# First block's attention: a pair's two heads multiply with the values in the two column halves of the array

## What is computed

```
q  = (rms_norm(c_q)  @ w_uq ).reshape(..., 8, 64 + 32)      # rope on the last 32
kv = (rms_norm(c_kv) @ w_ukv).reshape(..., 8, 64 + 64)      # k_nope, v
s  = (q_nope @ k_nope.T + q_rope @ k_rope.T) * 96 ** -0.5   # causal, the meta tokens always seen
p  = softmax(s)
out = p @ v                                                 # per head [256 queries, 64]
merged = concat(rms_norm(out of 8 heads), rms_norm(conv)) @ w_out
```

## Time and profile before

| | before |
|---|---|
| median of 3 runs | 684.5 us (684.24 to 686.52) |
| profiled execution, its span | 681.9 us |
| PE busy | 633.8 us (93%) |
| PE weight loads busy | 479.1 us (70%) |
| DVE busy | 356.7 us (52%) |
| ACT busy | 294.6 us (43%) |
| POOL busy | 51.3 us (8%) |
| DMA | 180.73 MB, mean 265 GB/s |

### The profile page before, as it was taken

The page is one execution under the profiler, slowest core; times in us unless marked ns, Lnnn a source line. Parts: engine busy times, 40 slices in busy tenths (PEclk is TensorE's granted clock), DMA queues, the critical chain, the costliest instruction groups (busy, mean ns, idle before and its releaser), DMA issues.

```text
span 681.9 us, 10213 instructions
## 1 busy us (share of the span) xinstructions
PE 633.8 (93%) x4027; PEld 479.1 (70%) x4027; DVE 356.7 (52%) x689; ACT 294.6 (43%) x562; POOL 51.3 (8%) x76
## 2 busy tenths in 40 slices
PE   8999899998998766879899999999999999999996
PEld 5979788842543320334389999998788888888884
DVE  5687664731031020110188876757856666666665
ACT  6855572431011010100185755564665555555554
POOL 3100101100010000000049000000000000000001
PEclk9999999999999997879999999999999999999999
DMA  8956328999999999999997333355535555555101
GB/s 341 420 227 245 130 118 346 395 382 426 426 389 424 421 420 420 422 421 420 423 420 295 131 125 124 124 186 186 185 128 193 193 195 194 200 194 186 62 1 62
DMA packets 26286, 180.73 MB, mean 265 GB/s; under 512 B 3184, under 2 KB 3312, under 8 KB 5120
## 3 DMA queue, kind: packets, MB, share of 16 engines
q1 hardware_dynamic: 25200, 177.60, 66.1%
q10 hardware_dynamic: 1040, 2.50, 0.9%
HBM read 179.04 MB, written 1.05 MB: 264 GB/s over the span
## 4 chain that ended last, share of the span: by engine, by line
PE 69%; DMA 16%; DVE 8%; ACT 5%; issue 2%; SPq 0%; POOLq 0%; POOL 0%; ACTq 0%; DVEq 0%
PE ps L1612 66%; DMA ring<-stream_dram 15%; PE ps L1615 3%; DVE ring_r L408 3%; ACT single L401 1%; DMA h<-x_dram 1%; DVE work L1547 1%; ACT work L887 1%; DVE work L1550 1%; DVE h L1600 0%; DVE work L1603 0%; ACT turned L892 0%; ACT work_r L883 0%; DVE extra_r L503 0%; DVE work L1428 0%
## 5 line engine op out<-in xcount | busy, mean ns | idle before, releaser
L1612 PE MATMUL ps<-turned,single 128*128 128x256 f32 (+2 forms) x944 | 231.2, 326 | 1.6 <-ACT work L664 0.8
L1612 PE MATMUL ps<-turned,ring_r 128*128 128x256 f32 (+1 forms) x648 | 179.7, 281 | 0.0
L1612 PEld LDWEIGHTS ps<-turned,single 128*128 128x128 f32 x944 | 156.2, 189 | 18.5 <-issue 2.0
L408 DVE TENSOR_TENSOR ring_r<-ring,single 128x1024 fp32r<-128x1024 f32 (+1 forms) x132 | 160.3, 1236 | 14.1 <-ACT single L401 13.9
L401 ACT ACTIVATE single<-ring 128x1024 fp32r<-128x1024 f32 (+1 forms) x132 | 134.0, 1046 | 0.1
L1612 PEld LDWEIGHTS ps<-turned,ring_r 128*128 128x128 f32 x648 | 121.1, 188 | 0.4
L1612 PE MATMUL ps<-ring,work 128*32 128x512 f32 (+2 forms) x462 | 69.9, 611 | 16.0 <-DMA ring<-stream_dram 13.9
L1612 PEld LDWEIGHTS ps<-single 128*128 128x128 f32 x257 | 38.7, 190 | 34.0 <-issue 22.8
L1612 PE MATMUL ps<-single,turned 128*128 128x512 f32 (+3 forms) x208 | 59.2, 364 | 2.4 <-DVE turned L1227 1.5
L1612 PE MATMUL ps<-single 128*128 128x512 f32 (+1 forms) x257 | 55.7, 356 | 2.9 <-DVE single L1439 1.9
L1612 PE MATMUL ps<-single,work_r 128*128 128x512 f32 x176 | 56.2, 392 | 0.0
(11 more groups left out here) (260 smaller groups left out, 719.1 us busy)
## 6 DMA issues: line engine op xcount, KB each, us to landing
ring<-stream_dram SPq DMA_DIRECT2D x145, 1024.0 KB, 12.4
work<-stream_dram SPq DMA_DIRECT2D x12, 1024.0 KB, 12.5
turned_w<-stream_dram SPq DMA_DIRECT2D x4, 1024.0 KB, 14.4
extra<-stream_dram SPq DMA_DIRECT2D x2, 1024.0 KB, 11.4
ring<-stream_dram SPq DMA_DIRECT2D x2, 832.0 KB, 8.4
h<-x_dram SPq DMA_DIRECT2D x2, 512.0 KB, 4.9
gain<-gains_dram ACTq DMA_DIRECT2D x2, 512.0 KB, 10.4
yields<-stream_dram SPq DMA_DIRECT2D x1, 1024.0 KB, 13.0
```

Source lines behind the costliest of these rows:

```text
L408: dve.tensor_tensor(ring_r[:, place, a], ring[:, place, a], w_hi[k % HIGHS][:, a].bitcast(F32), ALU.subtract).then_inc(s["wlo_done"], 1)
L1612: return pe.matmul(o, lhsT, rhs, start=start, stop=stop, **kw)
```

## The change

The values of a pair no longer have zeros between the heads: `v1` has one tile for each of the three key tiles (meta first), 64 columns for each head. `values(hp)` is called once for a pair. It multiplies head j's 64 columns to the rows 64 j to 64 j + 63 of the bank, with both query tiles streamed as 256 columns for the meta keys and the first 128 keys, and the second query tile alone (128 columns) for the last 128 keys: six fp32 matmuls, the two heads taking turns. The transposed probabilities of all four units of a pair are kept (`pt1` and the new `pt_meta`). `values(u // 4 - 1)` stands at u = 4, 8 and 12, ahead of `turn_probs(u)`, and that of the last pair behind the loop; what `turn_probs` cuts out of a row is shifted so that the meta keys come apart. POOL's three memsets and the waits on `pad_done` 2 go.

```diff
-            act.wait_ge(s["o_ps"], 4 * (hp + 1))
+            act.wait_ge(s["o_ps"], hp + 1)
...
-                        sp.wait_ge(s["o_ps"], 2 * HEADS)
+                        sp.wait_ge(s["o_ps"], HEADS // 2)
...
-                    if w == 0:
-                        act.wait_ge(s["pad_done"], 2)
                     act.wait_ge(s["pt_ps"], w + 1)
-                    full_k = P if w % 2 == 0 else 2 * P
-                    act.activation(pt1[:, w % 2, 0:full_k], ps[:, 3 + w % 2, 0:full_k], ACT.Copy)
-                    act.activation(pt1[0:META, w % 2, full_k:full_k + P], ps[0:META, 3 + w % 2, full_k:full_k + P],
+                    j, i = (w // 2) % 2, w % 2
+                    act.activation(pt1[:, j, i * P:(2 * i + 1) * P], ps[:, 3 + w % 2, 0:(i + 1) * P], ACT.Copy)
+                    act.activation(pt_meta[0:META, j, i * P:(i + 1) * P], ps[0:META, 3 + w % 2, 2 * P:3 * P],
                                    ACT.Copy).then_inc(s["pt_sb"], 1)
...
-            pool.memset(pm1[:, :, COLS:3 * P], 0.0).then_inc(s["pool_step"], 1)
...
-            pool.memset(pt1[:, 0, P:2 * P], 0.0).then_inc(s["pool_step"], 1)
...
-            pool.memset(pt1[:, 1, 2 * P:3 * P], 0.0).then_inc(s["pad_done"], 1)
...
-                for k in range(2 + u % 2):
-                    last = turn(ps[:, 3 + u % 2, k * P:(k + 1) * P], pm1[:, u % 3, k * P:(k + 1) * P])
+                for k in range(1 + u % 2):
+                    last = turn(ps[:, 3 + u % 2, k * P:(k + 1) * P], pm1[:, u % 3, META + k * P:META + (k + 1) * P])
...
-                last.then_inc(s["pt_ps"], 1)
-
-            def values(u):
-                hd, i = u // 2, u % 2
-                pe.wait_ge(s["pt_sb"], u + 1)
-                if hd >= 4 and u % 4 == 0:
-
-                    pe.wait_ge(s["att_low"], hd // 2 - 1)
-                o = ps[:, 6 + (hd // 2) % 2, i * P:(i + 1) * P]
-                c = (3 * (hd // 2) + hd % 2) * VD
-                for k in range(2 + i):
-
-                    last = mm(o, v1[k][:, c:c + 2 * VD], pt1[:, i, k * P:(k + 1) * P], u % 4 == k == 0,
-                              u % 4 == 3 and k == 1 + i, skip_group_check=True)
+                turn(ps[:, 3 + u % 2, 2 * P:3 * P], pm1[:, u % 3, 0:P]).then_inc(s["pt_ps"], 1)
+
+            def values(hp):
+
+                pe.wait_ge(s["pt_sb"], 4 * hp + 4)
+                if hp >= 2:
+                    pe.wait_ge(s["att_low"], hp - 1)
+                for k in range(NT + 1):
+                    for j in range(2):
+                        c = (2 * hp + j) * VD
+                        probs = pt_meta[:, j, :] if k == 0 else pt1[:, j, (k - 1) * TOK:TOK + (k - 1) * P]
+                        last = mm(ps[j * VD:(j + 1) * VD, 6 + hp % 2, (k // 2) * P:TOK], v1[:, k, c:c + VD], probs,
+                                  k == 0, k == NT, skip_group_check=True)
                 last.then_inc(s["o_ps"], 1)
...
+                if u and u % 4 == 0:
+                    values(u // 4 - 1)
                 turn_probs(u)
-                if u:
-                    values(u - 1)
...
-            values(2 * HEADS - 1)
+            values(HEADS // 2 - 1)
```

More of the change, by code:

```diff
@@ L205, in two_blocks @@
         xn = cut(NT, D)
-        v1_last = cut(3 * VD * HEADS // 2)
+        pt_meta = cut(2, TOK)
         top[0] = (NT + 1) * D
@@ L218, in two_blocks @@
         kT = cut(HEADS, COLS)
-        v1_whole = cut(NT, 3 * VD * HEADS // 2)
-        v1 = [v1_whole[:, 0, :], v1_whole[:, 1, :], v1_last]
+        v1 = cut(NT + 1, VD * HEADS)
         assert top[0] <= ASIDE_FROM + 4 * SLOT
@@ L535, in two_blocks @@
         TILES = [(0, META, 0), (1, P, META), (2, P, META + P)]
+        VALUE_TILES = TILES[1:] + TILES[:1]
         block = ctx.enter_context(nc.Block())
@@ L691, in _ @@
             act.wait_ge(s["pad_done"], 1)
[L692 to L696, removed]
+            for j, (i, m, _) in enumerate(VALUE_TILES):
+                act.wait_ge(s["v_ps"], j + 1)
+                act.activation(v1[0:m, i, :], ps[0:m, 4 + j, :], ACT.Copy).then_inc(s["v_sb"], 1)
             for hp in range(0, HEADS // 2, 2):
@@ L964, in power @@
                 return pool.tensor_tensor(rs, ms, cst[:, C_NHALF:C_NHALF + 1].to_broadcast([P, rs.shape[1]]), ALU.pow)
-            for a, value in ((kT[QKD:P, :, :], 0.0), (ones_s, 1.0), (qT[QKD:P, :, :], 0.0), (v1_last, 0.0)):
+            for a, value in ((kT[QKD:P, :, :], 0.0), (ones_s, 1.0), (qT[QKD:P, :, :], 0.0), (pt_meta, 0.0)):
                 pool.memset(a, value).then_inc(s["pool_step"], 1)
@@ L969, in _ @@
                 pool.wait_ge(s["pool_step"], steps[0])
-            pool.memset(v1_whole, 0.0).then_inc(s["pad_done"], 1)
+            pool.memset(v1[:, 0, :], 0.0).then_inc(s["pad_done"], 1)
             pool.wait_ge(s["pad_done"], 1)
@@ L980, in _ @@
             power(msz, rsz).then_inc(s["rz_done"], 1)
-            pool.wait_ge(s["qr_done"], NT)
-            pool.wait_ge(s["t3_ps"], 3)
-            pool.memset(pm1[:, :, COLS:3 * P], 0.0).then_inc(s["pool_step"], 1)
-            steps[0] += 1
-            pool.wait_ge(s["pool_step"], steps[0])
-            pool.memset(pt1[:, 0, P:2 * P], 0.0).then_inc(s["pool_step"], 1)
-            steps[0] += 1
-            pool.wait_ge(s["pool_step"], steps[0])
-            pool.memset(pt1[:, 1, 2 * P:3 * P], 0.0).then_inc(s["pad_done"], 1)
             def add_squares(to, other):
@@ L1740, in _ @@
                 last.then_inc(s["q_ps"], 1)
-            for i, m in enumerate((P, P, META)):
-                pe.wait_ge(s["q_sb"], (1, 1, 2)[i])
-                mm(ps[0:m, 4 + i, :], ckvT[:, i * P:i * P + m], wkv[:, HEADS * NOPE:HEADS * (NOPE + VD)], True, True
+            for j, (_, m, c) in enumerate(VALUE_TILES):
+                pe.wait_ge(s["q_sb"], (1, 1, 2)[j])
+                mm(ps[0:m, 4 + j, :], ckvT[:, c:c + m], wkv[:, HEADS * NOPE:HEADS * (NOPE + VD)], True, True
                    ).then_inc(s["v_ps"], 1)
@@ L1765, in _ @@
             pe.wait_ge(s["v_sb"], 3)
-            pe.wait_ge(s["pad_done"], 2)
             def scores(u):
```

## The result

| | before | changed |
|---|---|---|
| median, five runs each on one chip | 684.46 us (683.67 to 686.52) | 688.19 us (686.43 to 688.59) |
| profiled execution, its span | 681.9 us | 684.6 us |

The changed kernel takes 1.0051 of the time before, with a 95% interval of 1.0037 to 1.0065: about 3.5 us slower. The forecast of 684.6 us, with a range up to 686.8, is wrong: 688.19 lies above it. An unchanged copy of the changed kernel on a second chip gave 1.0031 (1.0019 to 1.0042); the two intervals meet at 1.0037 to 1.0042. The profiled execution of after took 686.43 us and is the fastest of its five. It lies 1.8 us above its span, as in every profiled run for which both are known. So of the 2.6 us that the forecast put around the span of before only 1.8 lie there; the rest is scatter between executions.

The account below looks back on a forecast made before the run. PE was taken to bound the attention's second half, with waits in the first. Terms +0.28, -0.31, -0.62 and +0.73 sum to +0.08 us: span 682.0, plus 2.6 gives 684.6 us, range 682.8 to 686.8.

Parts of the forecast that it names:

- A block, 1.40 us: One pair's value matmuls on PE in column halves: 1.09 us plus 0.31 for switching parts, against 2.24 before.
- Term 1: Up to unit 4's transposes: values(1) and values(2) go (-1.12 us), block 0 comes (+1.40); conv_share start also later: +0.28.
- Term 2: 83.69 us to unit 13's transposes: values(6) to values(11) go, two blocks come, new wait of 0.25 us: -0.31 us.
- the clock falls: Rival: about 2.5 us idle ahead of conv_share lowers PE's clock in the attention; 686.3 to 688.0 us; chance 0.12.
- Term 3: Unit 13's to unit 15's transposes: values go, new wait of 0.5 us for unit 15's probabilities: -0.62 us.
- Term 4: End of the attention: the last block (1.40 us) stands where values(15) (0.67) stood, behind unit 15's copy: +0.73 us.
- (a): 48 value records in place of 80; those of 256 columns start in twos; a block takes 1.1 us without edges.
- (b): The first record behind a block comes 0.1 us late, and its transposes too.
- (d): PE waits 0.25 us ahead of unit 11's transposes and 0.5 us ahead of unit 15's.
- (c): The first conv_share starts at about 84.0 us in place of 83.69.
- (e): The last block starts about 1.14 us behind unit 15's transposes, and mix_share within 0.5 us of 105.8.
- All of it shows: Rival: switches cost nothing and the 4.6 us of PE work saved over four blocks all count; 679.9 us; chance 0.09.

Follow-up runs that it names:

- kernel 1: Changed kernel plus four unused fp32 matmuls of 272 columns in PE's idle time ahead of the first conv_share; 685.24 us, ratio 1.0006.
- kernel 8: kernel 7 with the third pair's block behind unit 15's transposes and ACT's and DVE's work on that pair behind it; 681.42 us, 0.9955.
- kernel 5: Kernel before, with values(5) moved from ahead of the first conv_share to behind it; 688.06 us, 1.0052.
- kernel 7: Changed kernel with a second buffer for turned probabilities, the first pair's block moved into the hole ahead of conv_share; 683.98 us, 0.9995.
- kernel 3: Changed kernel's order and streams, but values padded with zeros so each matmul takes the whole array, no halves; 689.3 us, 1.007.
- kernel 4: Kernel before plus three unused fp32 matmuls in its 1.54 us hole ahead of the first conv_share; 684.18 us, 0.9998.
- kernel 6: kernel 3 plus the four filler matmuls of kernel 1; 687.57 us, 1.005.
- kernel 9: Kernel before plus four unused fp32 matmuls of 128 columns around turn_hidden in the first expert group; 684.47 us, 1.0002.
- kernel 10: kernel 1 plus the extra matmuls in the first expert group; 684.37 us, 1.0006.
- kernel 11: kernel 8 plus the extra matmuls in the first expert group; 681.17 us, 0.9955.

## Why the prediction was wrong

**What bounds the kernel** was read rightly: from `mix_share` to 200 us every profile runs alike but for the fall at 151 us, so a shift of the attention's end is passed on whole. A lost clock in the attention is paid in full too.

**A block, 1.40 us:** measured from 72.56 to 73.80, 1.24 us, 1.38 with an entry of 0.09 and transposes that come 0.05 later. The 48 records are there (x12 in each block). That the halves run side by side like the quarters of the earlier trace rows is right; the cost of going in and out of them, taken as 0.31 from the earlier trace rows, is 1.38 - 1.09 = 0.29. The Trainium skill says that different tiles can execute loads and matmuls in parallel (TensorEngine Tiling (Array Packing), Key Properties); this case agrees, with 1.23 us for a block in halves against 2.17 for the same streams over the whole array.

**Term 1, +0.28:** `conv_part(8)` to unit 4's transposes took 11.07 us before and 73.80 - 62.50 = 11.30 after, +0.23. The start of `conv_share` came 20.73 us behind `conv_part(8)` against 20.49, +0.24.

**Term 2, -0.31:** this failed. Before it took 100.57 - 83.69 = 16.88 us, after 101.51 - 83.23 = 18.28, +1.40. With the hole filled it is 101.98 - 85.29 = 16.69, -0.19. **The step that failed is the one in term 1 that says that taking `values(3)` to `values(5)` out of the holes "gives nothing", together with the forecast's choice of a whole clock.** Work in a hole has no value as time, but it kept the hole at 1.54 us. What the runs showed in its place: with the hole at 2.2 us the clock fell to half for 3.4 us, and the attention took 1.6 us more. The rival "the clock falls" had the right place, mechanism and lower price (1.7 us for half a fall; runs gave 1.41 to 1.65), and was given 0.12. That its upper figure, 688.0, lies near the 688.19 measured is luck: it stood for one fall of 6.8 us, and what came in the profile was one of 3.4 us in each of two places.

The row that was counted against this rival spoke for it. PE had idled 3.75 us from 250 to 260 us at whole clock, but the fall comes behind such idle time, and it came. In the kernel before:

```profile
258.60 1.06 PE L1612 MATMUL ps<-ring,work 128*32 128x512 f32 x8 [1.43 <-DMA ring<-stream_dram]
261.08 1.94 PE L1612 MATMUL ps<-ring,work 128*32 128x512 f32 x8 [1.42 <-DMA ring<-stream_dram]
```

and by stretch (length, PE, PEld, DVE, ACT, POOL, clock, DMA share, GB/s):

```profile
261.00:264.00 3.00, 2.36 (x12) 0.40 (x16) 0.00 (x0) 0.00 (x0) 0.00 (x0) 0.51 1.00 418
```

Eight records of the same form take 1.94 us in place of 1.06. The rival foresaw a hole of about 2.5 us; it was 2.18, with 0.54 more ahead of unit 6's transposes.

**Term 3, -0.62:** 104.34 - 101.51 = 2.83 against 3.42, -0.59, and the new wait for DVE is there, 0.38 us (0.5 foreseen).

**Term 4, +0.73:** 106.74 - 104.34 = 2.40 against 1.83, +0.57. The block starts 1.17 us behind unit 15's transposes (1.14 foreseen) and takes 1.23 to `mix_share`, not 1.40, since the way into the halves lies behind that wait.

**The sum, +0.08:** with the clock whole, kernel 1 gives +0.04 for the interval and a ratio of 1.0006. With the clock held, each of the four terms is right within 0.16 us. In its own list of what would show it, (a), (b) and (d) hold; unit 11's transposes come 0.31 us late (0.25 foreseen). (c) foresaw `conv_share` 0.3 us late, which it is by 0.24. Of (e) the first half holds; `mix_share` within 0.5 us of 105.8 doesn't, it started at 106.74. (f), a clock of 1.00 from 84 to 106 us, is 0.94. And one of its signs of being wrong came true: 1.7 us of the profiled execution lie in the first expert group, a stage that the change doesn't touch.

**"All of it shows"** was rightly put aside for this order. The 3.4 us are in the change, though, and kernel 8, by moving two blocks and ACT's and DVE's work on one of them, ends the attention 2.8 us earlier than before.

**What stays open.** The change cost 3.5 us on one chip and 2.1 on the other; 1.6 is shown to be the fall in the attention. The rest isn't shown. In the first profile it is the fall at 151 us, and the table of clocks fits more lost clock in general, but can't say where it cost time. Of the four profiles with the large hole two had the fall in the first expert group (the change's first and kernel 5) and two didn't; kernel 7 had it without the large hole. Nor is it known what decides that the clock falls. At the first `conv_share` 0.20 to 1.57 us of idle time kept it, 2.18 to 2.21 lost it, and nothing between was run. But the length of one idle time can't be the whole rule: 0.73 us ahead of the first expert group's quarter matmuls was enough in three profiles of ten, and 1.42 us ahead of 261.08 us in the kernel before, where several such idle times follow each other.

## What to carry to other kernels

Before taking work out of an idle stretch of PE as worthless, add up how long the stretch becomes and look at what stands behind it: if PE-bound work does, a longer hole can cost more than the work did. Where DMA ends last, as in the experts' stage here, half clock costs little or nothing. Four matmuls that nobody reads took the change from 1.0031 to 1.0006 on the same chip, and real work in the same place, with the blocks where PE waits anyway, to 0.9955. And when a change saves PE work but not time, test it with the clock held first, since otherwise the two can't be told apart.

## What was not expected of the hardware

- **An idle time of 2.2 us was enough for the clock.** In the four profiles with 2.18 to 2.21 us idle ahead of the first `conv_share` (the change twice, kernels 3 and 5) PE's clock went to 1.2 GHz for 3.4 us, from 0.3 us before its restart to 0.8 us behind it. In kernel 5 it was the only idle time of more than 0.25 us since `conv_part(11)` began. In the nine profiles with 0.20 to 1.57 us (before, kernels 1, 4, and 6 to 11) the clock stayed at 2.4 GHz there; only two of them, before and kernel 9, had more than 1.0 us. In the matmuls that followed the fall cost 1.4 to 1.65 us each time.
- **Lost clock costs next to nothing where DMA ends last.** Half clock from 230 to 345 us, 24 us of it before and 31 in the changed kernel's profile, left the time from `mix_share` to the end the same within 0.1 us, once the 1.7 us at 151 us are taken off.
- **Fp32 matmuls on two column halves run fully side by side.** Two records of 256 columns, one of each head, start 0.01 us apart, and the next two follow 0.216 us later; a block takes 1.23 us against 2.17 over the whole array. Going in and out costs 0.29 us in all, where no wait stands ahead of the block.
- **A fall at a place that is alike in both kernels.** The 32 quarter-array matmuls of the first expert group took 3.64 us before, and 5.34 in three profiles of other kernels, behind an idle time of 0.73 or 0.74 us that all ten profiles without a filler there have.
